# Norms of features-first parts: sums of squares with tokens on partitions, root and reciprocal of two columns, rows by products with diagonals

## The reference

```python
def rms_norm(x, g):
    y = xf * lax.rsqrt(jnp.mean(xf * xf, axis=-1, keepdims=True) + EPS)
    return (y * g.astype(jnp.float32)).astype(x.dtype)

for l in range(2):                                   # first block
    h = modulate(rms_norm(x, ffn1_norm[l]), sh1, sc1)
    x = x + 0.5 * g1 * swiglu(h, ...)                # width 2816
    h = modulate(rms_norm(x, mix_norm[l]), sh2, sc2)
    x = x + g2 * mix(h)                              # pooling and attention, w_out
    h = modulate(rms_norm(x, ffn2_norm[l]), sh3, sc3)
    x = x + 0.5 * g3 * swiglu(h, ...)
x = rms_norm(x, final_norm)
# second block: h = rmsnorm(x, g_pre_mix), state space and attention mixer,
# then a gated feed-forward layer, each with a norm behind it
```

## Time and profile before

| | |
|---|---|
| median of 3 runs | 1300.24 us (1299.71 to 1301.41) |
| profiled execution | 1303.72 us, its span 1301.8 us |
| TensorE busy | 1269.5 us, 98% |
| VectorE busy | 998.9 us, 77% |
| ScalarE busy | 604.3 us, 46% |
| five sums of 128x256, one norm | 2.40 us |
| root of 128x256, one | 0.47 us |
| reciprocal of 128x256, one | 1.75 us |

### The profile page before, as it was taken

One profiled execution on the slowest core, in us unless ns is written; L12 is line 12 of the kernel. 1 busy time (PEld: TensorE's weight loads), 2 busy tenths in 40 slices (PEclk: granted clock), 3 DMA queues, 4 the chain that ended last, 5 costly groups with the idle time before them and its releaser, 6 DMA issues.

```text
span 1301.8 us, 25351 instructions
## 1 busy us (share of the span) xinstructions
PE 1269.5 (98%) x10727; PEld 1224.3 (94%) x10727; DVE 998.9 (77%) x1595; ACT 604.3 (46%) x864; POOL 88.8 (7%) x159
## 2 busy tenths in 40 slices
PE   8899999999999999999999999999999998999998
PEld 7899999999999999999999989999999987999997
DVE  3799998877888667999988877899966757655554
ACT  3543334566433636333345755333354566533333
POOL 0111110000011040111110000000001000000000
PEclk8999999999999999999999999999998999999999
DMA  9899998441888652999993425555523522444551
GB/s 369 352 382 376 360 355 313 138 154 35 319 341 306 244 197 114 359 362 353 352 383 116 162 82 193 196 191 196 211 85 115 195 65 82 178 179 179 193 195 49
DMA packets 66096, 293.83 MB, mean 226 GB/s; under 512 B 7744, under 2 KB 8896, under 8 KB 51904
## 3 DMA queue, kind: packets, MB, share of 16 engines
q1 hardware_dynamic: 47552, 225.10, 47.4%
q0 software_dynamic: 18432, 67.12, 12.9%
HBM read 291.14 MB, written 1.05 MB: 224 GB/s over the span
## 4 chain that ended last, share of the span: by engine, by line
PE 88%; DVE 6%; ACT 3%; issue 1%; DMA 1%; SPq 0%; DVEq 0%; ACTq 0%
PE gu_bank L611 16%; PE gu_bank L609 16%; PE gu_bank L610 16%; PE y_bank L609 7%; PE y_bank L610 7%; PE y_bank L611 7%; PE t_bank L609 2%; PE t_bank L610 2%; PE t_bank L611 2%; PE gu_bank L661 1%; PE gu_bank L662 1%; PE gu_bank L665 1%; DVE dn_lo L1738 1%; PE y_bank L635 1%; DVE rstdT L1687 1%
## 5 line engine op out<-in xcount | busy, mean ns | idle before, releaser
L609 PE MATMUL gu_bank<-hT_hi,gu_hi 128*128 128x256 f32 x1668 | 463.5, 278 | 3.5 <-DVE gu_lo L1752 1.7
L611 PE MATMUL gu_bank<-hT_hi,gu_lo 128*128 128x256 f32 x1668 | 463.3, 278 | 0.0
L610 PE MATMUL gu_bank<-hT_lo,gu_hi 128*128 128x256 f32 x1668 | 463.1, 278 | 0.0
L609 PEld LDWEIGHTS gu_bank<-hT_hi,gu_hi 128*128 128x128 f32 x1668 | 314.6, 189 | 5.1 <-issue 2.3
L610 PEld LDWEIGHTS gu_bank<-hT_lo,gu_hi 128*128 128x128 f32 x1668 | 314.8, 189 | 0.8
L611 PEld LDWEIGHTS gu_bank<-hT_hi,gu_lo 128*128 128x128 f32 x1668 | 314.7, 189 | 0.0
L1298 ACT ACTIVATE sg<-gu_bank 128x256 f32<-128x256 f32 x110 | 42.3, 385 | 495.2 <-PE gu_bank L611 495.2
L1743 DVE TENSOR_TENSOR gu_lo<-raw_gu,gu_hi 128x2048 fp32r<-128x2048 f32 x105 | 240.8, 2293 | 37.0 <-ACT gu_hi L1285 31.9
L1285 ACT ACTIVATE gu_hi<-raw_gu 128x2048 fp32r<-128x2048 f32 x100 | 191.1, 1911 | 14.5 <-DMA raw_gu<-ffn_gu 14.5
L1637 DVE SCALAR_TENSOR_TENSOR stage<-stage,c_row 128x1024 f32<-128x1024 f32 x128 | 150.6, 1220 | 0.0
L609 PE MATMUL y_bank<-act_hi,dn_hi 128*128 128x256 f32 x528 | 146.4, 277 | 2.0 <-DVE act_lo L1778 2.0
(11 more groups left out here) (473 smaller groups left out, 2238.5 us busy)
## 6 DMA issues: line engine op xcount, KB each, us to landing
raw_gu<-ffn_gu SPq DMA_DIRECT2D x110, 1024.0 KB, 6.3
stage<-ada POOLq DMA_DIRECT2D x128, 512.0 KB, 7.8
raw_dn<-ffn_dn SPq DMA_DIRECT2D x110, 512.0 KB, 3.7
ring<-mix_w SPq DMA_DIRECT2D x72, 512.0 KB, 3.6
stage<-ada SPq DMA_DIRECT2D x8, 512.0 KB, 14.7
pro<-ada SPq DMA_DIRECT2D x6, 512.0 KB, 13.9
x<-x_in SPq DMA_DIRECT2D x1, 1024.0 KB, 5.5
ring<-ada SPq DMA_DIRECT2D x2, 512.0 KB, 17.7
```

What stands on the lines that cost most here:

```text
L609: pe.matmul(to, a[0], b[0], start=start, stop=False)
L610: pe.matmul(to, a[0], b[1], start=False, stop=False)
L611: return pe.matmul(to, a[1], b[0], start=False, stop=stop)
```

## The change

For norms 1 to 6 the sums are made with the tokens on the partitions. The squares are now the weights (128 features x 128 tokens, two halves of 128 tokens) and one column of ones is the moving operand. The result is two columns of 128 tokens (128x2), in the bank where the row was. A product of two columns of zeros clears them first. Chunk 4 is taken ahead of chunk 0. Root and reciprocal act on 128x2 (`rms`, `rstd`). VectorE then multiplies the 128x128 identity by each column (`diagonals`, into the memory of `rstdT` or `rmsT`), and TensorE multiplies ones by each diagonal (`rows_for`), which gives the row of 128x256 on all partitions, in PSUM. `scaled` reads it there. The fillers are divided: two ahead of the rows and three (two in norm 6) behind them, where six or seven stood. In norm 6 the rows of the final norm follow behind the products by chunk and are copied to `rstdT`, and `col_tile(3)` waits for that copy. Norm 0 keeps its form.

```diff
@@ tensor @@
+            def token_sums(to, squares_, c, last):
+                for t in range(TT):
+                    done = pe.matmul(to[:, t:t + 1], squares_[:, c, tok(t)], ones[:, 0:1], start=False, stop=last and t == TT - 1)
+                return done
+            def clear_columns(to):
+                pe.matmul(to[:, 0:TT], zero[:, 0:1].to_broadcast([P, P]), zero[:, 0:1].to_broadcast([P, TT]), start=True, stop=False)
             def sums(kt):
...
-                pe.wait_ge(part_done, kt)
-                for c in (0, 4, 5, 6, 7):
-                    if c:
-                        pe.wait_ge(sq_done, KC * kt + c + 1)
-                    last = pe.matmul(to, ones[:, :], sq_x[:, c, :], start=c == 0, stop=c == KC - 1)
+                clear_columns(to)
+                for c in (4, 0, 5, 6, 7):
+                    pe.wait_ge(*((sq_done, KC * kt + c + 1) if c else (part_done, kt)))
+                    last = token_sums(to, sq_x, c, c == KC - 1)
                 last.then_inc(ss_ps, 1)
+            def rows_for(to, src, first, signal):
+                for t in range(TT):
+                    pe.wait_ge(norm_diag, first + t + 1)
+                    last = pe.matmul(to[:, tok(t)], ones[:, :], src[:, t, :], start=True, stop=True)
+                last.then_inc(signal, 1)
             def sums_of_both():
...
+                for to in (ss_bank(NORMS), gu_bank[1]):
+                    clear_columns(to)
+                for w, c in ((0, 4), (0, 0), (1, 4), (0, 5), (1, 5), (1, 0), (0, 6), (1, 6), (0, 7), (1, 7)):
...
-                busy(7)
+                busy(2)
+                rows(3 * l + 1)
+                busy(3)
                 mixer(l)
                 pe.wait_ge(tile_out, TILES * (l + 1))
                 busy(4)
                 sums(3 * l + 2)
-                busy(6)
+                busy(2)
+                rows(3 * l + 2)
+                busy(3)
                 for bank_ in gu_bank:
                     clear(bank_)
...
-                    busy(6)
-                    pe.wait_ge(rms_ready, 3 * l + 4)
+                    busy(2)
+                    rows(3 * l + 3)
+                    busy(3)
...
             pe.wait_ge(fms_ready, 1)
-            busy(6)
+            busy(2)
+            rows_for(mix_rows_ps, diag, TT * (NORMS - 1), norm_rows)
+            busy(2)
...
+                if n == 3:
+                    pe.wait_ge(last_rows_out, 1)
...
             by_chunk(NORMS, [(to, lambda c, w=w: [a[:, tok(c)] for a in w], True, True, tile_ps) for to, w in tiles])
+            rows_for(last_rows_ps, last_diag, TT * NORMS, last_rows)
@@ scalar @@
-                act.activation(rmsT[:, :], ss_bank(kt), ACT.Sqrt, bias=eps, scale=1.0 / D).then_inc(rms_ready, 1)
+                    act.activation(rms[:, :], ss_bank(kt)[:, 0:TT], ACT.Sqrt, bias=eps, scale=1.0 / D).then_inc(rms_ready, 1)
@@ vector @@
+                step.then(dve.reciprocal(rstd[:, :], rms[:, :]))
+                diagonals(last_diag if kt == NORMS else diag, rstd)
+            def diagonals(to, by):
+                for t in range(TT):
+                    dve.tensor_scalar(to[:, t, :], ident, by[:, t:t + 1], None, ALU.mult).then_inc(norm_diag, 1)
...
             def normed(kt):
                 root(kt)
+                dve.wait_ge(norm_rows, kt)
                 for c in range(KC):
-                    scaled(kt, c, rstdT[:, :])
+                    scaled(kt, c, rows_ps)
...
-            root(NORMS)
+            dve.wait_ge(last_rows, 1)
+            dve.tensor_copy(rstdT[:, :], last_rows_ps).then_inc(last_rows_out, 1)
+            dve.wait_ge(last_rows_out, 1)
```

More of the change, by code:

```diff
@@ L309, in program @@
         post_sq, post_rooted = sem("post_sq"), sem("post_rooted")
+        norm_diag, norm_rows, last_rows, last_rows_out = sem("norm_diag"), sem("norm_rows"), sem("last_rows"), sem("last_rows_out")
         block = ctx.enter_context(nc.Block())
@@ L393, in program @@
         mix_bank = (*yb[2:], *tb)
+        diag, last_diag = (a[:, :].rearrange("p (t n) -> p t n", t=TT) for a in (rstdT, rmsT))
+        rows_ps, mix_rows_ps, last_rows_ps = yb[3][:, 0:S], tb[1][:, S:2 * S], tb[1][:, 0:S]
         HT_STEPS = (0, 1, 2, 4, 6)
@@ L568, in sums, with rows @@
                     pe.wait_ge(prod_done, FB * (2 * (kt // 3) + (kt % 3 > 0)) - 1)
-                pe.wait_ge(part_done, kt)
-                for c in (0, 4, 5, 6, 7):
-                    if c:
-                        pe.wait_ge(sq_done, KC * kt + c + 1)
-                    last = pe.matmul(to, ones[:, :], sq_x[:, c, :], start=c == 0, stop=c == KC - 1)
-                last.then_inc(ss_ps, 1)
-            def sums_of_both():
[L578 to L584, removed]
+                clear_columns(to)
+                for c in (4, 0, 5, 6, 7):
+                    pe.wait_ge(*((sq_done, KC * kt + c + 1) if c else (part_done, kt)))
+                    last = token_sums(to, sq_x, c, c == KC - 1)
+                last.then_inc(ss_ps, 1)
+            def rows(kt):
+                rows_for(rows_ps, diag, TT * (kt - 1), norm_rows)
+            def rows_for(to, src, first, signal):
[3 more added lines that the diff above has]
+                last.then_inc(signal, 1)
+            def sums_of_both():
+                for to in (ss_bank(NORMS), gu_bank[1]):
+                    clear_columns(to)
+                for w, c in ((0, 4), (0, 0), (1, 4), (0, 5), (1, 5), (1, 0), (0, 6), (1, 6), (0, 7), (1, 7)):
+                    to, squares_, ready, first = ((ss_bank(NORMS), sq_x, sq_done, KC * NORMS), (gu_bank[1], hT, fsq_done, 0))[w]
+                    pe.wait_ge(*((ready, first + c + 1) if c else (fpart_done, 1) if w else (part_done, NORMS)))
+                    last = token_sums(to, squares_, c, c == KC - 1)
+                    if (w, c) == (0, KC - 1):
                         last.then_inc(ss_ps, 1)
-                    last = pe.matmul(gu_bank[1][:, 0:S], ones[:, :], hT[:, c, :], start=c == 0, stop=c == KC - 1)
                 last.then_inc(fss_ps, 1)
@@ L1210, in root @@
                 act.wait_ge(ss_ps, kt + 1)
-                act.activation(rmsT[:, :], ss_bank(kt), ACT.Sqrt, bias=eps, scale=1.0 / D).then_inc(rms_ready, 1)
+                if kt == 0:
+                    act.activation(rmsT[:, :], ss_bank(kt), ACT.Sqrt, bias=eps, scale=1.0 / D).then_inc(rms_ready, 1)
+                else:
+                    act.activation(rms[:, :], ss_bank(kt)[:, 0:TT], ACT.Sqrt, bias=eps, scale=1.0 / D).then_inc(rms_ready, 1)
             def shifted(kt):
@@ L1474, in _ @@
             act.wait_ge(fms_ready, 1)
-            act.activation(ma[:, 1, :], ma[:, 0, :], ACT.Sqrt, bias=tiny[:, 1:2], scale=1.0 / D).then_inc(frms_ready, 1)
+            act.activation(ma[:, 1, 0:TT], ma[:, 0, 0:TT], ACT.Sqrt, bias=tiny[:, 1:2], scale=1.0 / D).then_inc(frms_ready, 1)
             root(NORMS)
@@ L1686, in root @@
                 dve.wait_ge(rms_ready, kt + 1)
-                step.then(dve.reciprocal(rstdT[:, :], rmsT[:, :]))
+                if kt == 0:
+                    step.then(dve.reciprocal(rstdT[:, :], rmsT[:, :]))
+                    return
+                step.then(dve.reciprocal(rstd[:, :], rms[:, :]))
[3 more added lines that the diff above has]
+                    dve.tensor_scalar(to[:, t, :], ident, by[:, t:t + 1], None, ALU.mult).then_inc(norm_diag, 1)
             def scaled(kt, c, by):
@@ L2207, in _ @@
             dve.wait_ge(ss_ps, NORMS + 1)
-            step.then(dve.tensor_scalar(ma[:, 1, :], ss_bank(NORMS), EPS, None, ALU.mult))
+            step.then(dve.tensor_scalar(ma[:, 1, 0:TT], ss_bank(NORMS)[:, 0:TT], EPS, None, ALU.mult))
             dve.wait_ge(fss_ps, 1)
-            dve.tensor_tensor(ma[:, 0, :], gu_bank[1][:, 0:S], ma[:, 1, :], ALU.add).then_inc(fms_ready, 1)
+            dve.tensor_tensor(ma[:, 0, 0:TT], gu_bank[1][:, 0:TT], ma[:, 1, 0:TT], ALU.add).then_inc(fms_ready, 1)
             dve.wait_ge(frms_ready, 1)
-            step.then(dve.reciprocal(ma[:, 1, :], ma[:, 1, :]))
+            step.then(dve.reciprocal(ma[:, 1, 0:TT], ma[:, 1, 0:TT]))
+            diagonals(diag, ma[:, 1, 0:TT])
+            root(NORMS)
+            dve.wait_ge(norm_rows, NORMS)
             def mix_lo(c):
@@ L2218, in _ @@
             for c in range(KC):
-                scaled(NORMS, c, ma[:, 1, :])
+                scaled(NORMS, c, mix_rows_ps)
                 if c:
```

## The result

The changed kernel takes 1304.14 us (median, 1300.87 to 1306.49), the kernel before 1301.16 us (1298.74 to 1304.94): a ratio of 1.0022, interval 1.0012 to 1.0033. In a second series it was 1.0033 (1.0023 to 1.0044). So it is slower by 3 to 4 us, where 3.35 us less were forecast. The profiled execution took 1304.83 us with a span of 1302.6.

A forecast was written before the change was run, and what follows sets the result against it. TensorE, 98% busy, was taken as the bound, with gains where it waits at the norms: 2 x 1.11 + 0.65 + 2 x 0.20 + 0.08 = 3.35 us. Adjusted to the median of the runs: 1296.9 us, range 1295.0 to 1301.0.

The forecast's parts named there:

- The sums: Norms' sums: passes 0.11 us apart, no shorter; start and order give 0.47 us at norms 1 and 4.
- Root to scaling: From the end of a norm's sums to its scaling: 1.69 us where 2.33 were, 0.64 less.
- TensorE behind the diagonals: Rows products, fillers and clearings bound norms 2, 3, 5; gains 1.11 (norms 1, 4), 0.65 (3), 0.20 (2, 5), 0.08 (6).
- No wait for hT_hi at norms 2, 3 and 5: Sign in the changed profile: the first product behind these norms no longer waits for hT_hi.
- Clock 1.00 throughout: Sign in the changed profile: TensorE's granted clock stays at 1.00; 0.50 beside any norm would be wrong.
- rivals 1 and 2: Clock falls at the sixth norm, 1300.2 us, chance 0.16; or at several norms, 3.35 us each, chance 0.12.
- the fall at 999.0: Warning in the earlier trace: behind narrow products from 990 to 999 the clock fell to 0.50 until 1005.7, costing 3.35 us.
- Rival 2: Clock falls at several norms after one-column sums, 3.35 us each; three falls give 1306.9 us; chance 0.12.
- The price of a fall: Cost assumed for each clock fall at a norm: 3.35 us, from 6.7 us at half speed in the earlier trace.
- Rival 3: One-column passes of the sums run closer than 0.11 us; at half of it 1291.5 us; chance 0.05.
- Rival 4: Gains of norms 1 and 4 are lost inside the mixer: 1296.9 + 2.2 = 1299.1 us; chance 0.10.

The follow-up runs named there:

- 128-column kernel: The changed kernel with 128 columns of ones instead of one as moving operand of each sum: 1295.86 us against 1299.57 for the kernel before, ratio 0.9968.
- 128 columns at norm 6: The changed kernel with 128 columns of ones in the sums of norm 6 alone: 1300.94 us against 1300.95 for the kernel before, ratio 1.0006.
- 128 columns at norms 1 to 5: The changed kernel with 128 columns of ones in the sums of norms 1 to 5, one column at norm 6: 1301.40 us, ratio 1.0004.
- norms 1 to 5 only: The changed kernel with norm 6 left in the form of before: 1299.30 us against 1299.91 for the kernel before, ratio 0.9994.
- before, fewer fillers: The kernel before with two fillers instead of four ahead of norms 2 and 5's sums, chunk 4 ahead of chunk 0 at norms 1 to 5: 1298.83 us, 0.9982.
- the fastest kernel: The changed kernel with 128 columns of ones in all sums and fewer fillers at norms 2, 3, 5 and 6: 1291.81 us against 1299.91, ratio 0.9941.

## Why the prediction was wrong

The forecast was 1296.9 us, the result 1304.14, above the range. Step by step:

- **The sums.** Right. Passes 0.11 apart; clearing and 20 passes in 2.26 us (2.31 said), and they start 0.11 behind the last product (219.90 and 220.01), as said (220.04 and 220.15). The 0.47 for start and order at norms 1 and 4 is found by itself in the kernel before with chunk 4 first: 0.48 and 0.62.
- **Root to scaling.** From the root's start 1.65 said (1.69 less the hand-over ahead), 1.58 measured. The two multiplications last 0.48 us, not 0.55.
- **TensorE behind the diagonals.** The gains without a fall are 1.25, 0.33, 0.77, 1.25 and 0.33 for norms 1 to 5 where 1.11, 0.20, 0.65, 1.11 and 0.20 were said. For norm 6 the 128-column kernel has 0.45 where 0.52 was said, and four passes of rows behind it (980.02 to the transposes at 980.47 in the changed kernel) 0.45 for 0.44. The chain's sum is 3.9 us, a little better than the 3.35 of the forecast. At norms 1 and 4 the text let the chain decide (225.55) and had TensorE free at 225.41, 1.25 us earlier than 226.66; 1.25 is what was won, so the chain was at least 0.14 shorter than said.
- **No wait for hT_hi at norms 2, 3 and 5.** Right, and norms 1 and 4 have none either. The one left is at norm 6; the waits of TensorE, after, answer to the earlier trace rows:

```profile
PE gu_bank L681 <- ACT hT_hi L1514: 0.2, 1, 0.2
```

- **"Clock 1.00 throughout".** This is the step that failed: the sum has no term for the clock. The runs show falls worth 9.2 us by the mean clock against 3.9 us of gain. The text had it as rivals 1 and 2, chances 0.16 and 0.12, and argued against them that dense work stands on both sides, that gaps of 0.54 cost no clock, and that narrow products in the earlier trace rows ran at full clock for most of 9 us. None of these carried over to one-column passes. The warning in the same rows, the fall at 999.0, pointed the right way partly by luck: over 13 traces that fall goes with a gap of TensorE (below), and six traces have the same narrow products without it. Rival 2's mechanism is the true one, and its count (three falls) is what the first trace has.
- **The price of a fall.** 3.35 us was taken from a fall of 6.7 us. At norms 1 to 5 a fall lasts 3.3 to 3.4 us and costs 1.2 to 1.7 us; at norm 6 it cost 1.6 once and 3.3 once, against the 128-column kernel's 10.44. Three falls at the price of rival 2 gave 1306.9; about five at the smaller price (9.2 us by the mean clock) less 3.9 us of gain would be 5.3, where 4.3 were measured.
- **Rival 3** (passes closer than 0.11) is out. Rival 4 is out in its size: the mixers give back 0.06 us each here and 0.2 to 0.3 on average, not 1.1.

Between the two profiled executions the five stages between the norms are even (705.15 us in both). The norms take 0.4 more with their three falls (46.03 and 46.44), the part ahead of norm 1 takes 0.1 less, and the part behind norm 6 0.6 more. That is the longer span, within 0.1. The 0.6 is a sum of several things: 0.45 for the rows, a gap at the second block's inputs that is 1.9 us longer, and against them a fall at 1060.4 to 1063.9 that only the kernel before has. So the two spans alone show no cause.

What an account by mean clock gives, in us against the kernel before on the same chip (chain: the table's sums and the rows of norm 6; clock: mean clock of the executions times the span):

| kernel | chain | clock | together | measured |
|---|---|---|---|---|
| changed, second series | -3.9 | +9.2 | +5.3 | +4.3 |
| 128 columns everywhere | -3.4 | -0.8 | -4.2 | -4.2 |
| 128 columns at norm 6 | -3.9 | +4.2 | +0.3 | +0.8 |
| 128 columns at norms 1 to 5 | -3.4 | +3.7 | +0.3 | +0.5 |
| norms 1 to 5 only | -3.9 | +4.0 | +0.1 | -0.8 |
| before, fewer fillers | -2.4 | +0.2 | -2.2 | -2.3 |

Measured is the ratio less 1, times 1300. The clock of one execution is given to 0.001, and the falls outside the norms vary too, so 1 us either way is not told apart; the first and the fifth row miss by that much, and that is left open. How much they vary: ahead of norm 1, where all kernels have the same work, the 13 traces have a clock of 0.50 for between 0 and 17 us, and norm 1 begins between 217.1 and 222.3 us. Norm 6 with one column was never seen without a fall, so its chain is taken from the 128-column kernel.

**What stays open.** Some executions have one more fall, behind TensorE's gap in the second block's first products. The page calls the gap "issue": nothing that the profile shows was waited for. It was 3.2 us in the changed kernel's first trace and 1.3 before:

```profile
PE y_bank L1061 <- issue: 3.2, 1, 3.2
```

```profile
PE y_bank L1032 <- issue: 1.3, 1, 1.3
```

Of the 13 traces, the seven with a gap of 1.2 us or more there have a clock of 0.50 behind it, for 3.4 or 6.8 us. The six with no gap or 0.2 us have none. Five of the seven have the new form at norm 6, but so does the fastest kernel, which has no gap. Whether the change makes the gap likelier can't be said from one trace of each. It isn't tied to one-column passes: the kernel with 128 columns everywhere and the kernel before have it too.

## What to carry to other kernels

A product of one column costs TensorE the same 0.11 us a pass as one of 128 columns with the same f32 weights, but it can cost the clock: 2.2 us of such passes lost it in 10 of 22 cases as sums and in 2 of 6 as fillers, 4.4 us in all three. If a sum by products has to stand on TensorE, give its moving side columns that cost no time, and read the copy that is wanted. Try the order of the waits by itself before the new form: here it gave a good part of the gain, and its trace has no fall at any norm. And price a chain's gain on TensorE only together with the granted clock of every stretch that becomes thin: the busy share stays at 100% through a fall, and only the clock's column and the lengths of records show it.

## What the runs showed of the hardware

- One-column passes: 20 in 2.24 us, as 20 of 128 columns in 2.24 us. The fall comes behind them or among them and not with their first: at norm 3 at 497.7, 2.9 us behind the first pass, when dense fillers had begun at 497.01; at norm 6 at 965.3, 4.3 us behind the first.
- With the clock at 0.50 the 16 transposes of norm 6 and the hand-over behind them took 3.25 us (965.64 to the filler at 968.89); in the 128-column kernel 1.75. At norms 1 and 4, where the chain over VectorE and ScalarE sets part of the time, a fall of 3.4 us costs 1.2 to 1.3, elsewhere 1.5 to 1.7.
- Transposes of 128x128 f32, 36 on end, keep the clock at 1.00.
- The changed kernel's slowest execution, 1306.49 us, has the lowest mean clock, 0.982; the one with the highest, 0.989, took 1301.84. The number of falls in an execution is a source of spread of its own.
